# Opening of a two-block transformer kernel: rows taken as they come, a modulation load moved to TensorE

## The reference

```python
cs = jax.nn.silu(c)
mod = cs @ w_ada[l] + b_ada[l]                 # [1024] @ [1024, 6144]
sh1, sc1, g1, sh2, sc2, g2 = jnp.split(mod, 6)
h = rms_norm(x, norm1_g[l]) * (1.0 + sc1) + sh1
q, k, v, gu, gv, ga, gb = jnp.split(h @ w_in[l], splits, axis=-1)
```

## Time and profile before

| | |
|---|---|
| median of 3 runs | 2945.87 us (2945.11 to 2948.99) |
| the profiled execution | 2952.91 us, of which the span is 2951.2 |
| PE busy | 2829.1 us, 96% of the span |
| PEld, DVE, ACT, POOL busy | 2360.0, 2235.7, 1479.3, 588.9 us |
| mean granted clock of TensorE | 0.981 of full speed |
| DMA | 737.92 MB, mean 250 GB/s |

### The profile page before, as it was taken

One profiled execution on the slowest core, in us unless ns is written; L12 is line 12 of the kernel. 1 busy time (PEld: TensorE's weight loads), 2 busy tenths in 40 slices (PEclk: granted clock), 3 DMA queues, 4 the chain that ended last, 5 costly groups with the idle time before them and its releaser, 6 DMA issues.

```text
span 2951.2 us, 37305 instructions
## 1 busy us (share of the span) xinstructions
PE 2829.1 (96%) x13639; PEld 2360.0 (80%) x13639; DVE 2235.7 (76%) x3019; ACT 1479.3 (50%) x1987; POOL 588.9 (20%) x460
## 2 busy tenths in 40 slices
PE   6989988999999989999999999999999999999998
PEld 4767756888888868776777789999999988888887
DVE  7455647888888863796954599999877658888886
ACT  4343235888888843444552434565766533333332
POOL 0110111111111100000000000233433324444442
PEclk7999998999999999999999999999999999999999
DMA  8654536999999843232334224688988999999995
GB/s 309 184 190 157 185 130 240 368 370 367 365 354 359 308 152 112 97 120 86 103 122 149 100 86 155 235 305 300 365 314 311 326 328 359 363 366 346 364 375 174
DMA packets 201772, 737.92 MB, mean 250 GB/s; under 512 B 24432, under 2 KB 77808, under 8 KB 145008
## 3 DMA queue, kind: packets, MB, share of 16 engines
q1 hardware_dynamic: 124656, 497.12, 46.7%
q0 software_dynamic: 55056, 170.87, 16.8%
q10 hardware_dynamic: 21872, 67.48, 5.9%
HBM read 666.61 MB, written 93.91 MB: 258 GB/s over the span
## 4 chain that ended last, share of the span: by engine, by line
PE 62%; DVE 14%; issue 4%; ACT 3%; DMA 2%; ACTq 0%; DVEq 0%; SPq 0%; POOLq 0%; POOL 0%
PE PS L544 54%; DVE wlo L1900 3%; PE PS L1154 2%; PE PS L1020 1%; ACT whi L1230 1%; DVE hf L2717 1%; PE PS L1032 1%; PE PS L854 1%; DVE hf L2705 1%; DVE oh L2691 1%; ACT HH L1870 1%; DVE zo L2428 1%; DVE cand L2654 1%; DVE cand L2652 1%; PE PS L1011 1%
## 5 line engine op out<-in xcount | busy, mean ns | idle before, releaser
L1900 DVE TENSOR_TENSOR wlo<-raw,whi 128x2048 fp32r<-128x2048 f32 x392 | 894.5, 2290 | 291.5 <-ACT whi L1230 270.8
L1230 ACT ACTIVATE whi<-raw 128x2048 fp32r<-128x2048 f32 x392 | 750.8, 1916 | 361.7 <-PE PS L544 310.7
L544 PE MATMUL PS<-HH,whi 128*128 128x512 f32 (+1 forms) x2056 | 788.4, 383 | 21.5 <-ACT HH L1266 10.9
L544 PE MATMUL PS<-HH,wlo 128*128 128x512 f32 (+1 forms) x2056 | 751.6, 366 | 0.0
L544 PE MATMUL PS<-HL,whi 128*128 128x512 f32 (+1 forms) x2056 | 751.1, 365 | 0.0
L544 PEld LDWEIGHTS PS<-HH,whi 128*128 128x128 f32 x2056 | 390.4, 190 | 84.1 <-issue 20.4
L544 PEld LDWEIGHTS PS<-HL,whi 128*128 128x128 f32 x2056 | 390.4, 190 | 46.5 <-issue 7.4
L544 PEld LDWEIGHTS PS<-HH,wlo 128*128 128x128 f32 x2056 | 389.6, 189 | 43.5
L544 PE MATMUL PS<-whi,HH 128*128 128x512 f32 (+1 forms) x896 | 351.5, 392 | 12.1 <-DVE HL L2749 6.8
L544 PE MATMUL PS<-wlo,HH 128*128 128x512 f32 (+1 forms) x896 | 347.4, 388 | 0.0
L544 PE MATMUL PS<-whi,HL 128*128 128x512 f32 (+1 forms) x896 | 347.3, 388 | 0.0
(11 more groups left out here) (434 smaller groups left out, 3895.7 us busy)
## 6 DMA issues: line engine op xcount, KB each, us to landing
raw<-in_moe_dram SPq DMA_DIRECT2D x192, 1024.0 KB, 7.3
raw<-in_u_units_dram SPq DMA_DIRECT2D x64, 1024.0 KB
raw<-in_v_units_dram SPq DMA_DIRECT2D x64, 1024.0 KB
raw<-in_w_in_dram SPq DMA_DIRECT2D x44, 1024.0 KB
raw<-in_w_ada_dram SPq DMA_DIRECT2D x24, 1024.0 KB, 22.3
acts_dram<-sS ACTq DMA_DIRECT2D x64, 384.0 KB
gates_dram<-XT ACTq DMA_DIRECT2D x24, 1024.0 KB
sS<-acts_dram SPq DMA_DIRECT2D x42, 384.0 KB, 7.0
```

What stands on the lines that cost most here:

```text
L544: ins = t.matmul(dst, a, b, start=(first and n == 0), stop=(last and n == 2))
L1230: a.inc(a.e.activation(m.whi[p % HRING][:, :, :], m.raw[RAW_SLOT[load_of(p)]][:, :, :], ACT.Copy), "hi", p)
L1900: v.inc(v.e.tensor_tensor(m.wlo[h][:, :, :], m.raw[RAW_SLOT[load_of(p)]][:, :, :], m.whi[h][:, :, :].bitcast(F32), ALU.subtract), "lo_v", p)
```

## The change

- `pe_project_rows` does weight unit 0: the loop over rows is outside, the loop over the four token tiles inside, so each row is used for all four tiles when it comes. The tick is after each row. Unit 1 goes through `pe_project` with `begun=1`.
- ht gets eight places (`nx`: four in gvN, four in qT), hf four (in guT). VectorE's order becomes low kc, then nx kc + 2; the low part of weight unit 0 comes after sg1 and that of unit 1 after row 3's.
- The modulation's load 7 goes from VectorE to TensorE (`pe_modulation_rows`), 16 products with one column of c. The place of that load is freed by `modp` 3.
- `pe_fill`, a product of ones by sq into bank 0 that nobody reads, stands twice ahead of load 7's products, once after each four of them, and three times after the last closing sum.

```diff
+            self.nx = [t[:, k, :] for t in (self.gvN, self.qT) for k in range(4)]

+def pe_project_rows(pe, m, p, hi, lo, inputs, tick):
+    h = pe_unit(pe, p)
+    for c in range(4):
+        inputs(c)
+        for j in range(4):
+            s = slice(128 * j, 128 * j + 128)
+            ins = mm3(pe.e, m.PS[:, j, :], m.whi[h][:, c, :], m.wlo[h][:, c, :], hi[:, c, s], lo[:, c, s], c == 0, False,
+                      w_moves=True)
+        if c == 3:
+            pe.inc(ins, "use", p)
+            pe.also("used", p)
+        tick(p, c)

+def pe_fill(pe, m):
+    pe.e.matmul(m.PS[:, 0, :], m.ones[:, :], m.sq[:, 0, :], start=True, stop=True)
+
+PE_ADA = {1: 0, 7: 3}
+
+def pe_modulation_rows(pe, m, i, side):
+    load, nb = LOAD_OF["w_ada", i], i // 2
+    pe.wait_ge("silu_c")
+    pe.wait_ge(raw_sem(load), load)
+    for j in range(4):
+        for c in range(4):
+            kc = 4 * (i % 2) + c
+            pe.e.matmul(m.PS[:, 6, 4 * nb + j:4 * nb + j + 1], m.raw[RAW_SLOT[load]][:, c, 128 * j:128 * j + 128],
+                        m.col("c")[:, kc:kc + 1], start=(j == 0 and c == 0), stop=False)
+        side(j)
 def pe_modulation(pe, m, nb):
+    begun = nb in (0, 2, 3)
+    pe.wait_ge("ada", 2 * nb if nb in (0, 3) else 2 * nb + 1)
     pe.wait_ge("const", "ones")
     for j in range(4):
+        ins = pe.e.matmul(m.PS[:, 6, 4 * nb + j:4 * nb + j + 1],
+                          m.acc[nb if nb < 4 else nb % 2][:, 128 * j:128 * j + 128], m.ones[:, 0:1],
+                          start=not begun, stop=(nb != 2 and j == 3) or not begun)
     pe.inc(ins, "modp", nb)
...
 def pe_first(pe, m):
     pe_sum_squares(pe, m, 0, ("const", "ones"))
-    for nb in range(4):
-        pe_modulation(pe, m, nb)
+    pe_modulation_rows(pe, m, 1, lambda j: None)
+    pe_modulation(pe, m, 0)
+    pe_modulation(pe, m, 1)
+    for _ in range(2):
+        pe_fill(pe, m)
+    pe_modulation_rows(pe, m, 7, lambda j: pe_fill(pe, m))
+    pe_modulation(pe, m, 2)
+    pe_modulation(pe, m, 3)
+    for _ in range(3):
+        pe_fill(pe, m)
...
-    pe_project(pe, m, "gv", places("w_in", 0, 2), "N", m.HH, m.HL, h1, none, tick)
+    pe_project_rows(pe, m, 0, m.HH, m.HL, h1, tick)
+    pe_project(pe, m, "gv", places("w_in", 1, 1), "N", m.HH, m.HL, h1, None, tick, begun=1)
...
 act_first, the loop over the rows:
-            i = kc % 2
+            i = kc % 4
             a.wait_ge("nx", 0, kc)
-            if kc > 1:
-                a.wait_ge("xlo", 1, kc - 2)
+            if kc > 3:
+                a.wait_ge("xlo", 1, kc - 4)
...
 dve_first:
+    normed(0, 1)
+    for i in range(4, 7):
         dve_modulation(v, m, i)
-    dve_low(v, m, 0)
     v.wait_ge("modp", 3)
...
+    dve_low(v, m, 0)
     for kc in range(KC):
-        if kc + 2 < KC:
-            normed(kc + 2)
-        dve_split_input(v, m, 1, kc, m.hf[:, kc % 2, :])
+        dve_split_input(v, m, 1, kc, m.guT[:, kc % 4, :])
+        if kc < 6:
+            normed(kc + 2)
+        if kc == 3:
+            dve_low(v, m, 1)
...
-    dve_project(v, m, "gv", places("w_in", 0, 2), None, tick)
+    for _ in range(4):
+        tick()
+    dve_project(v, m, "gv", places("w_in", 1, 1), None, tick)
```

More of the change, by code:

```diff
@@ L550, in pe_unit, with pe_project @@
     return p % HRING
-def pe_project(pe, m, name, ps, form, hi, lo, inputs, empty, tick=None):
+def pe_project_rows(pe, m, p, hi, lo, inputs, tick):
[10 more added lines that the diff above has]
+        tick(p, c)
+def pe_project(pe, m, name, ps, form, hi, lo, inputs, empty, tick=None, begun=0):
     t = pe.e
-    for g, p in enumerate(ps):
+    for g, p in enumerate(ps, begun):
         h = pe_unit(pe, p)
@@ L564, in pe_project @@
                 inputs(kc)
-                first, last = (g == 0 and c == 0), (g == len(ps) - 1 and c == 3)
+                first, last = (g == 0 and c == 0), (g == begun + len(ps) - 1 and c == 3)
                 s = slice(128 * j, 128 * j + 128)
@@ L572, in pe_project @@
                               first, last, w_moves=True)
-            if g == len(ps) - 1:
+            if g == begun + len(ps) - 1:
                 pe.inc(ins, "bank", name, j)
@@ L591, in pe_sum_squares @@
                "ssq", r, kc)
-def pe_modulation(pe, m, nb):
[L597 to L605, removed]
+def pe_fill(pe, m):
[11 more added lines that the diff above has]
+        side(j)
+def pe_modulation(pe, m, nb):
+    begun = nb in (0, 2, 3)
+    pe.wait_ge("ada", 2 * nb if nb in (0, 3) else 2 * nb + 1)
     pe.wait_ge("const", "ones")
     for j in range(4):
[L608 to L612, removed]
+        ins = pe.e.matmul(m.PS[:, 6, 4 * nb + j:4 * nb + j + 1],
+                          m.acc[nb if nb < 4 else nb % 2][:, 128 * j:128 * j + 128], m.ones[:, 0:1],
+                          start=not begun, stop=(nb != 2 and j == 3) or not begun)
     pe.inc(ins, "modp", nb)
@@ L750, in modulate @@
             pe_modulation(pe, m, 4 + (p - ADA_FROM) // 2)
-    none = [("const", "ones")] * 4
-    pe_project(pe, m, "gv", places("w_in", 0, 2), "N", m.HH, m.HL, h1, none, tick)
+    pe_project_rows(pe, m, 0, m.HH, m.HL, h1, tick)
+    pe_project(pe, m, "gv", places("w_in", 1, 1), "N", m.HH, m.HL, h1, None, tick, begun=1)
     pe_project(pe, m, "gu", places("w_in", 2, 2), "T", m.HH, m.HL, h1, [("ev", "gv", j) for j in range(4)], tick)
@@ L1331, in act_first @@
         if kc < KC:
-            i = kc % 2
+            i = kc % 4
             a.wait_ge("nx", 0, kc)
-            if kc > 1:
-                a.wait_ge("xlo", 1, kc - 2)
-            a.inc(s.activation(m.hf[:, i, :], m.ht[:, i, :], ACT.Identity, scale=m.sg1[:, kc:kc + 1],
+            if kc > 3:
+                a.wait_ge("xlo", 1, kc - 4)
+            a.inc(s.activation(m.guT[:, i, :], m.nx[kc], ACT.Identity, scale=m.sg1[:, kc:kc + 1],
                                bias=m.mod[:, kc:kc + 1]), "ha", 0, kc)
@@ L1339, in act_first @@
             a.wait_ge("ha", 0, kc - 1)
-            act_split_input(a, m, 1, kc - 1, m.hf[:, (kc - 1) % 2, :])
+            act_split_input(a, m, 1, kc - 1, m.guT[:, (kc - 1) % 4, :])
     side = act_bias(a, m)
@@ L2076, in dve_first, with normed @@
     side = dve_bias(v, m)
[L2078 to L2081, removed]
+    def normed(*kcs):
+        for kc in kcs:
+            v.inc(e.tensor_tensor(m.nx[kc], m.XT[:, kc, :], m.rstd[:, :], ALU.mult), "nx", 0, kc)
     dve_modulation(v, m, 0)
@@ L2087, in dve_first @@
     dve_inverse(v, m, 0)
-    normed(0)
-    normed(1)
-    for i in range(4, 8):
+    normed(0, 1)
+    for i in range(4, 7):
         dve_modulation(v, m, i)
-    dve_low(v, m, 0)
     v.wait_ge("modp", 3)
@@ L3080, in sync_load @@
         kind, i = LOADS[RAW_BEFORE[n]]
-        if kind == "w_ada" and i == 1:
-            y.wait_ge("modp", 0)
+        if kind == "w_ada" and i in PE_ADA:
+            y.wait_ge("modp", PE_ADA[i])
         elif kind == "w_ada":
```

## The result

| | before | after |
|---|---|---|
| median, ten runs each | 2946.31 us (2944.14 to 2953.36) | 2957.88 us (2949.76 to 2968.08) |
| ratio to before, 95% interval | | 1.0035 (1.0024 to 1.0046), +10.3 us (+7.1 to +13.6) |
| profiled execution, its span | 2952.91, 2951.2 | 2949.76, 2948.0 |
| mean granted clock in it | 0.981 | 0.986 |

The changed kernel is slower, and its runs spread twice as widely: 18.3 us against 9.2. One thing has to be read with care: the profiled execution of after is the fastest of its ten, while that of before, 2952.91, is slower than nine of its ten.

The account below looks back on a forecast made before the run. TensorE, 62% of the chain that ended last, was taken to bound the kernel, mostly a stream of matmuls. 52.8 + 22.1 - 63.04 + 1.9 = +13.8 us on the median 2945.87 gave 2959.7, range 2950.5 to 2962.

Parts of the forecast that it names:

- S: Moment in the opening when ScalarE starts the first row: 44.19 before, forecast at 52.8 with TensorE's clock low.
- my own signs: Opening: wrong if mod stands before 44, the TensorE gap is missing, or the clock is high from about 35 on.
- VectorE's last sum at 38.44, TensorE last: Modulation: without load 7 VectorE's last sum ends 3.17 us sooner, from 41.61, and TensorE's queue then sets S.
- Low clock, S = 52.8: Modulation on TensorE: clock stays low through products of ones, load 7 and closing sums; S 52.8, 2957 to 2962, chance 0.47.
- the high one: Rival, modulation on TensorE: clock stays high through all of load 7; S 44.7, 2949.7 to 2951.6, chance 0.14.
- The rise and fall in the middle: Rival, modulation on TensorE: clock rises in the first two products of ones, then falls; S 46 to 50, chance 0.29.
- One bound of mine: TensorE's start: raising the clock needs over 5.3 us of close work, as the weight load at 18.67 still took 0.34.
- Turn of 2.75 us, bias products at S + 22.1: Rows: nx joins the ScalarE-VectorE turn, 2.75 us against 2.22; second-half bias products can go at S + 22.1.
- The stop of about 7 us at the bias bank: After row 2's products TensorE waits some 7 us for the bias bank, which ScalarE empties only after all rows.
- Restart, 1.9 us: TensorE after the stop: products at half speed for 2.9 to 5.3 us lose 1.4 to 2.7, taken as 1.9.
- Nothing gives it back: After the opening: nothing returns the loss in full; later waits, such as 1.65 us at 99.00, could absorb up to that.

Follow-up runs that it names:

- nx_early: Changed kernel, with VectorE making all eight nx before it waits for the closing sums, not one after each split; 1.0003 to before, +0.9 us.
- after_again: The changed kernel run once more with no edit, for a second profile; 1.0029 to before, +8.5 us.
- load_only: Kernel before with only the modulation part: load 7 and the products of ones on TensorE, rows as before; 1.0005 to before, +1.5 us.
- copy_early: Changed kernel, with ScalarE emptying the bias bank after row 4's hf inside its row loop, not after all rows; 1.0005 to before, +1.5 us.
- rows_only: Kernel before with only the rows' part: load 7 stays on VectorE, no products of ones; 1.0007 to before, +2.1 us.
- nx_copy: Changed kernel with all nx made before the closing sums and ScalarE emptying the bias bank right after the rows; 1.0000 to before.

## Why the prediction came out as it did

The forecast was slower by 13.8 us with a range of +4.6 to +16.1 around the median before; measured were +10.3 and +8.5. The mechanism held from S on; which clock there would be was given as one case where the runs show two, and the size was too large, by a third against the first figure and by 60% against the second. By my own signs the first profile says wrong: mod stood at 40.75, before 44, and the clock was high from 32. The second, with mod at 49.19, a stop of 8.09 and the low clock, says right.

- **VectorE's last sum at 38.44, TensorE last:** 37.96, then a wait of 2.79 or 11.66 us for TensorE. Right; none of the six profiles with the change's products of ones had S below 40.98. In nx_early, where S was 40.98, VectorE's own nx came last.
- **Low clock, S = 52.8:** this was the term that failed in size. The low case was 49.64 in after_again and 49.74 in load_only, 51.99 and 52.49 in two others. The short products before it, which I let end at 31.5 as in the earlier trace rows, ended at 28.5 in the first two and at 30.9 and 31.3 in the others: they began up to 1.2 us sooner than the 23.54 of before, and in the first two the clock fell up to 1.1 us later (25.9 before). From the end of those short products to S the sum was right within 0.2 us in all four. The prices behind it were right: 1.71 for eight short products, and two closing sums in 3.41 against my 3.57.
- **Which case:** I gave 0.47 to the low case and 0.14 to the high one, and took the low one alone for the sum. Of six profiles with the change's products of ones, four are of the low case, two of the high one. In the high case S was 41.0 and 41.2, not 44.7, again as the first stretch ended sooner. The rise and fall in the middle was not seen once: a clock that was up stayed up through the half-filled stretch. One bound of mine is not sure: that the clock was still low at 18.67 in before I read from a weight load's length, and the granted-clock column shows 1.00 there.
- **Turn of 2.75 us, bias products at S + 22.1:** 2.82 and S + 22.57. Right; nx inside the turn, and nx_early takes it out.
- **The stop of about 7 us at the bias bank:** 9.17 and 8.09. Right, and copy_early takes it away with one edit and some 8 us of the time with it.
- **Restart, 1.9 us:** 73.60 - 63.78 = 9.82 against 7.07 before, 2.75 lost, at the upper end of what I gave (2.7). After_again lost 2.67, rows_only 1.8. The Trainium skill, TensorE: Matmul & The Clock Gate (HAM oscillation — how this bites in real kernels), says that waits between bursts throttle the array again so that each burst starts cold; the bias products at 0.50 of the clock after the stop agree.
- **Nothing gives it back:** this was the second term off. The stop of 1.65 at 99.00 disappears when TensorE comes later: between the bias steps around it lie 6.06 us before, 4.52 after. I had left it at zero with 1.65 as the bound; 1.5 is what it gave. With 12.3 for the low case and some 4 for the high one, at even odds, the sum would have been 8, close to the 8.5 of the second set. That account uses the same runs and is a reading, not a test. The steps themselves give less: at the ninth group the changed kernel is 2.0 behind before in one profile and 10.1 in the other, 6 on the average, where the times say 8.5 and 10.3. Before's opening is known from one execution, slower than nine of its ten, and where the other 2 to 4 us lie stays open.

For the low case of after_again the terms add up: 13.8, less 3.2 for S, plus 0.5 for the way from S to the bias products, plus 0.8 for the restart, is 11.9, and the third bias step was 11.8 behind. That the median fell 1.8 us from the forecast 2959.7 is in part luck: it is a mixture of a case above and a case below. The range held because the other clock was in it as a rival. Its end on the side of no change, 2950.5, is close to the fastest runs. I called it the upper end of the no-change case, but by my own sums that rival reached 2951.6 and the 5.9 us of no change 2951.8.

## What to carry to other kernels

Work that fills a wait belongs behind the last thing somebody is waiting for, not ahead of it: the products of ones were to use TensorE's waits, and the six of them ahead of the closing sums made TensorE the last of three engines. When a loop is turned round so that an engine comes earlier, look at every wait in its queue that the old order met just in time; here one copy on ScalarE, ready before just when TensorE came, stopped it for 9 us. And take a producer's helper step (nx) out of the turn between two engines when giving it more buffers: with eight places and one nx after each split the splits stood 2.8 us apart, with all made ahead 1.2.

## What the runs showed of the hardware

- The same instruction stream settles at either clock. In after the clock had fallen at about 28.6 and rose at about 32.0, behind two close products that began at 28.4; in after_again it had fallen at about 26.7, and the same products from 28.5 did not raise it: it stayed at 0.50 until 54. Once up it was held by a stretch filled half with short products and half with long ones (1.00 at 36 to 38); once down the same stretch did not raise it (0.50 at 34 to 36 and at 44 to 46).
- With the products of ones the runs spread over 18.3, 18.1 and 21.3 us (after, after_again, load_only), but over 11.7, 10.1 and 11.3 in copy_early, nx_early and nx_copy, which have them too. Without any they spread over 7.7 to 11.4, and before over 9.2 to 12.6. So the spread alone doesn't tell the two cases; the groups of nx_copy do. A kernel whose start hangs on the clock needs more than one profile to be judged: the only one at hand at first was its best case.
- Behind the opening the kernels run the same program, and its time there varies by as much as the effects here: from the ninth group of bias products to the end of the span the fourteen profiles took 2838.5 to 2846.5 us.
